# One word and the first rows ahead of the branch, and the MLP weights converted in pairs

## What is computed

```
h = RMSNorm(x);  [gB|gC|xA|xL|gL] = h @ w_in              # 1024 -> 5 x 512
outA = gB * conv3(gC * xA)                                # mixer A
outB = RG_LRU(conv4(xL) + b) * gelu(gL)                   # mixer B: h_t = a_t h_{t-1} + b_t
x = x + concat([outA, outB]) @ w_out
x = x + relu(RMSNorm(x) @ w_up)^2 @ w_down                # 4096 hidden columns
y = RMSNorm(x)
```

## Time and profile before

| | |
|---|---|
| median of 3 runs | 910.05 us (909.71 to 910.27) |
| the profiled execution | 909.05 us |
| its slowest core, 6 | span 907.5 us |
| even cores (0, 2, 4, 6) | 903.0 to 907.5 us |
| odd cores (1, 3, 5, 7) | 899.8 to 902.1 us |
| TensorE busy on core 6 | 839.3 us (92%) |
| VectorE, ScalarE, GpSimd | 425.2, 376.3, 184.9 us |
| queue of GpSimd's DMAs, share of 16 engines | 23.2% (33.30 MB) |
| queue of SyncE's DMAs | 42.4% (111.76 MB) |

### The profile page before, as it was taken

The page is one execution under the profiler, slowest core; times in us unless marked ns, Lnnn a source line. Parts: engine busy times, 40 slices in busy tenths (PEclk is TensorE's granted clock), DMA queues, the critical chain, the costliest instruction groups (busy, mean ns, idle before and its releaser), DMA issues.

```text
span 907.5 us, 15041 instructions; the slowest of 8 cores (899.8 to 907.5 us)
## 1 busy us (share of the span) xinstructions
PE 839.3 (92%) x4392; PEld 428.5 (47%) x4464; DVE 425.2 (47%) x722; ACT 376.3 (41%) x754; POOL 184.9 (20%) x307
## 2 busy tenths in 40 slices
PE   2679789699999999999999999999999899999995
PEld 2444345255564444444444444555445455446542
DVE  4698886663301210636665434575315477514112
ACT  4578738552331000554942134583205485205301
POOL 4132240234453000232100013120003212003200
PEclk9799889899999999999999999999999999999998
DMA  8999999999888534685553369565248852778751
GB/s 237 205 180 215 214 117 130 134 180 177 163 182 168 145 96 126 241 318 172 141 149 84 117 164 300 163 166 161 84 151 254 267 159 73 233 198 271 206 163 73
DMA packets 80441, 158.26 MB, mean 174 GB/s; under 512 B 9184, under 2 KB 9312, under 8 KB 80352
## 3 DMA queue, kind: packets, MB, share of 16 engines
q1 hardware_dynamic: 61632, 111.76, 42.4%
q0 software_dynamic: 15264, 33.30, 23.2%
q10 hardware_dynamic: 3456, 12.14, 4.1%
HBM read 165.75 MB, written 32.57 MB: 219 GB/s over the span
## 4 chain that ended last, share of the span: by engine, by line
PE 82%; DMA 8%; DVE 4%; issue 3%; ACT 2%; POOL 0%; POOLq 0%; DVEq 0%; ACTq 0%; SPq 0%
PE ps L1037 28%; PE ps L1087 27%; PE ps L780 12%; PE ps L989 7%; DMA sb_ring<-wscr 4%; PE ps L776 3%; DMA sb_uT<-wall 3%; PE ps L1079 2%; PE ps L697 1%; PE ps L1097 1%; DMA sb_xsl<-xp 1%; PE ps L855 1%; ACT sb_t_rig L532 1%; PE ps L1074 1%; DVE sb_t_xc L882 1%
## 5 line engine op out<-in xcount | busy, mean ns | idle before, releaser
L1037 PE MATMUL ps<-sb_hT,sb_ring 128*128 128x512 bf16 (+2 forms) x1050 | 194.3, 341 | 6.2 <-DVE sb_a_pb L535 4.3
L532 ACT ACTIVATE sb_junk<-sb_xsl 128x1024 bf16<-128x1024 f32 (+1 forms) x59 | 59.6, 1010 | 269.7 <-DVE sb_xsl L535 256.6
L535 POOL TENSOR_TENSOR sb_uT<-sb_rl 128x512 bf16<-128x512 bf16 (+1 forms) x80 | 83.0, 1038 | 418.4 <-ACT sb_stat L532 272.7
L532 ACT ACTIVATE sb_rl<-ps 128x512 bf16<-128x512 f32 (+2 forms) x192 | 98.1, 525 | 142.2 <-PE ps L1037 127.8
L1037 PEld LDWEIGHTS ps<-sb_hT,sb_ring 128*128 128x128 bf16 x1064 | 104.4, 99 | 91.3 <-issue 8.4
L535 DVE TENSOR_TENSOR sb_xsl<-ps,sb_xsl 128x512 f32<-128x512 f32 (+1 forms) x60 | 46.1, 794 | 200.7 <-PE ps L1087 139.9
L1087 PE MATMUL ps<-sb_ring,sb_uT 128*128 128x512 bf16 x576 | 138.5, 379 | 0.8
L1087 PE MATMUL ps<-sb_uS,sb_uT 128*128 128x512 bf16 x423 | 95.7, 379 | 0.5
L1037 PE MATMUL ps<-sb_hT,sb_uS 128*128 128x512 bf16 (+1 forms) x466 | 92.6, 354 | 0.3
L1087 PEld LDWEIGHTS ps<-sb_ring,sb_uT 128*128 128x128 bf16 x592 | 57.6, 98 | 67.8
L780 PE MATMUL ps<-sb_hT,sb_ring 128*128 128x512 bf16 (+1 forms) x369 | 81.8, 367 | 5.0 <-DMA sb_ring<-wscr 4.6
(11 more groups left out here) (100 smaller groups left out, 841.7 us busy)
## 6 DMA issues: line engine op xcount, KB each, us to landing
sb_ring<-wscr SPq DMA_DIRECT2D x240, 256.0 KB, 3.5
sb_uS<-wscr SPq DMA_DIRECT2D x160, 256.0 KB, 3.0
wscr<-wall POOLq DMA_DIRECT2D x64, 256.0 KB, 10.8
sb_xsl<-xp ACTq DMA_DIRECT2D x18, 512.0 KB, 8.7
yp<-sb_xsl POOLq DMA_DIRECT2D x13, 512.0 KB, 7.9
sb_uT<-wall POOLq DMA_DIRECT2D x16, 256.0 KB, 24.1
wscr<-sb_uT SPq DMA_DIRECT2D x16, 256.0 KB, 14.4
sb_wout<-wout POOLq DMA_DIRECT2D x4, 512.0 KB, 13.1
```

Of the source, the lines that this page charges most:

```text
L532: return OP("act", dur, lambda e: e.activation(out=out, in_=in_, func=func, **kw), rd_, wr_)
L535: return OP(eng, dur, lambda e: e.tensor_tensor(out=out, in0=in0, in1=in1, op=op), rd_, wr_)
L1037: return lambda slot: [lambda e, kc=kc: e.matmul(out=bank_ap(b, q.N), lhsT=slot[:, kc * 128:(kc + 1) * 128], rhs=h_ap(q, True, kc, 0, q.N) ...
```

## The change

1. **Ahead of the branch.** `W.lead` emits the first instruction of `g_par` (the load of `par`) and the first of the new `g_head` (1 MB of rows) before anything else. `cut` holds how many entries of each engine's program these are; `emit` puts them between the read of the word and the branch. On ScalarE these are two DMAs, on the other engines nothing.
2. **The first rows.** A new input `head` (128 x 6144) holds the first 3 MB of rows in the order in which they are used: on even cores the two blocks of S and the four of M0, on odd cores the 2 MB of L0 and the two blocks of S. It is loaded by four DMAs (1, 1, 0.5 and 0.5 MB) in place of six on even cores (2 of `xs`, 4 of `xp`), and of four on odd cores.
3. **Pairs.** The chunks of `w_up` and `w_down` lie in `wall2` as 32 pairs of 128 x 2048 with rows padded to 2064, and are converted to the scratch `wscr2` by one DMA each. Both chunks of a pair share one buffer in the planner. Ring loads still take one chunk, now as rows of 2 KB at a stride of 4 KB. The planner's size of such a transfer is 0.94 for a pair instead of 0.52 for a chunk. The chunks of `w_in` and `w_out` stay as they are.

```diff
         def f(e):
+            n = cut[name]
             r = e.alloc_register("side")
             e.reg_load(r, side[0:1, 0:1])
+            put(e, arms[0].prog[name][:n])
             with e.If_eq(r, 0):
-                put(e, name, arms[0])
+                put(e, arms[0].prog[name][n:])
...
+        for i in range(CH_UP + 1, NCHUNK, 2):
+            scr_b[i] = scr_b[i - 1]
...
+        def scr_ap(chunk):
+            p, h = divmod(chunk - CH_UP, 2)
+            return wscr[chunk] if chunk < CH_UP else wscr2[p, :, h * 1024:(h + 1) * 1024]
...
-                S.dma("sp", ap, wscr[chunk], [scr_b[chunk]], [buf], "ring")
+                S.dma("sp", ap, scr_ap(chunk), [scr_b[chunk]], [buf], "ring")
...
-                    yield DMA("pool", wscr[chunk], wall[chunk, :, 0:1024], [], [scr_b[chunk]], "cv", 0.52)
+                    p = (chunk - CH_UP) // 2
+                    yield DMA("pool", wscr2[p], wall2[p, :, 0:2048], [], [scr_b[chunk]], "cv", 0.94)
...
+        def g_head():
+            for k in range(6):
+                P_x.free.remove(k)
+            for k, n in ((0, 2), (2, 2), (4, 1), (5, 1)):
+                yield DMA("act", xsl[:, k * D:(k + n) * D], head[:, k * D:(k + n) * D], [], [xsl_b[k + i] for i in range(n)], "x", 0.52 * n)
...
-            for t in chain:
+            for t in chain[2:]:
...
-        W.spawn(g_conv(order), 500)
+        setup, conv, pars, rows = g_setup(), g_conv(order), g_par(), g_head()
+        for gen, n in ((pars, 1), (rows, 1)):
+            W.lead(gen, n)
+        cut = {e: len(S.prog[e]) for e in S.ENG}
```

More of the change, by code:

```diff
@@ L143, in check_no_deadlock, with emit, put @@
             raise RuntimeError("static deadlock: " + "; ".join(msg))
-def emit(nc, arms, side):
-    def put(e, name, S):
-        for waits, fns, inc in S.prog[name]:
+def emit(nc, arms, cut, side):
+    def put(e, part):
+        sem = arms[0].sem
+        for waits, fns, inc in part:
             for k, v in waits:
-                e.wait_ge(S.sem[k], v)
+                e.wait_ge(sem[k], v)
             ins = None
@@ L156, in put @@
             if inc is not None:
-                ins.then_inc(S.sem[inc[0]], inc[1])
+                ins.then_inc(sem[inc[0]], inc[1])
     def make(name):
         def f(e):
+            n = cut[name]
             r = e.alloc_register("side")
             e.reg_load(r, side[0:1, 0:1])
+            put(e, arms[0].prog[name][:n])
             with e.If_eq(r, 0):
-                put(e, name, arms[0])
+                put(e, arms[0].prog[name][n:])
             with e.Else():
-                put(e, name, arms[1])
+                put(e, arms[1].prog[name][n:])
         return f
@@ L355, in _emit, with lead @@
                 b.tw = land
+    def lead(self, gen, n):
+        s, val = Strand(gen, -99, 0), None
+        pace, self.PACE = self.PACE, {}
+        while n:
+            s.req, val = gen.send(val), None
+            if s.req[0] == "get":
+                val = s.req[1].take(s.req[2])
+            else:
+                self._emit(s, self._start(s.req))
+                n -= 1
+        self.PACE = pace
     def run(self):
@@ L381, in dout @@
         return nc.dram_tensor(name, list(shape), dt, kind="ExternalOutput").ap()
-    xp, xl, xs = din("xp", [NF, D]), din("xl", [128, 8 * NF]), din("xs", [256, D])
+    xp, xl, head = din("xp", [NF, D]), din("xl", [128, 8 * NF]), din("head", [128, 6 * D])
     side_d = din("side", [1, 1], mybir.dt.int32)
-    wall = din("wall", [NCHUNK, 128, WPAD])
+    wall = din("wall", [CH_UP, 128, WPAD])
+    wall2 = din("wall2", [(NCHUNK - CH_UP) // 2, 128, 2 * 1024 + 16])
     wout_d = din("wout", [128, 8 * 1024])
@@ L391, in build_program @@
     stp_d, sts_d = dout("stp", [128, 24]), dout("sts", [128, 96])
-    wscr = nc.dram_tensor("wscr", [NCHUNK, 128, 1024], BF16).ap()
+    wscr = nc.dram_tensor("wscr", [CH_UP, 128, 1024], BF16).ap()
+    wscr2 = nc.dram_tensor("wscr2", [(NCHUNK - CH_UP) // 2, 128, 2 * 1024], BF16).ap()
     es = ExitStack()
@@ L641, in arm @@
         Ms = tiles("M", xp, SECOND if second_half else FIRST, 20, 10, yp)
-        Ss = mk_tile("S", "S", xs, 0, 256, 4, 1.5, ys, 0)
+        Ss = mk_tile("S", "S", head, 0, 256, 4, 1.5, ys, 0)
         Ms[-1].last = True
@@ L645, in arm @@
         chain = Ls[0:1] + [Ss] + Ls[1:] + Ms
+        assert [t.J if not t.lean else 4 for t in chain[:2]] in ([4, 2], [2, 4])
         def xap(k):
@@ L650, in xap @@
             return xsl[:, k * D:(k + 1) * D]
+        def g_head():
[3 more added lines that the diff above has]
+                yield DMA("act", xsl[:, k * D:(k + n) * D], head[:, k * D:(k + n) * D], [], [xsl_b[k + i] for i in range(n)], "x", 0.52 * n)
+            if second_half:
+                Ls[0].xs, Ss.xs = {0: [0, 1], 1: [2, 3]}, {0: 4, 1: 5}
+            else:
+                Ss.xs, Ms[0].xs = {0: 0, 1: 1}, {0: 2, 1: 3, 2: 4, 3: 5}
+            for t in chain[:2]:
+                for _ in t.xs:
+                    W.mark("x" + t.name)
         def g_xloads():
-            for t in chain:
+            for t in chain[2:]:
                 for u in range(t.loads if t.lean else 0):
@@ L1165, in g_state @@
             out_events.append(S.last_dma)
-        order = [12, 13, 14, 15] + [16, 8, 4, 0, 17, 9, 5, 1, 18, 10, 6, 2, 19, 11, 7, 3] + list(range(CH_UP, NCHUNK))
-        W.spawn(g_setup(), -20)
-        W.spawn(g_conv(order), 500)
-        W.spawn(g_par(), -19)
-        W.spawn(g_xloads(), -10)
+        order = [12, 13, 14, 15] + [16, 8, 4, 0, 17, 9, 5, 1, 18, 10, 6, 2, 19, 11, 7, 3] + list(range(CH_UP, NCHUNK, 2))
+        setup, conv, pars, rows = g_setup(), g_conv(order), g_par(), g_head()
+        for gen, n in ((pars, 1), (rows, 1)):
+            W.lead(gen, n)
+        cut = {e: len(S.prog[e]) for e in S.ENG}
+        for gen, prio in ((setup, -20), (conv, 500), (pars, -19), (rows, -11), (g_xloads(), -10)):
+            W.spawn(gen, prio)
         W.spawn(g_norm1s(), -1)
@@ L1188, in arm @@
         S.check_no_deadlock()
-        return S, W
+        return S, W, cut
     with es:
         arms = [arm(False), arm(True)]
-        emit(nc, [a[0] for a in arms], side_d)
+        emit(nc, [a[0] for a in arms], arms[0][2], side_d)
+        assert arms[0][2] == arms[1][2]
     return nc, arms[0][1], arms[1][1]
@@ L1215 @@
     shared = {
-        "wall": f(np.pad(wall, ((0, 0), (0, 0), (0, WPAD - 1024)))), "wout": f(f(w_out[0]).reshape(8, 128, 1024).transpose(1, 0, 2).reshape(128, 8192)),
+        "wall": f(np.pad(wall[:CH_UP], ((0, 0), (0, 0), (0, WPAD - 1024)))),
+        "wall2": f(np.pad(wall[CH_UP:].reshape(-1, 2, 128, 1024).transpose(0, 2, 1, 3).reshape(-1, 128, 2048), ((0, 0), (0, 0), (0, 16)))),
+        "wout": f(f(w_out[0]).reshape(8, 128, 1024).transpose(1, 0, 2).reshape(128, 8192)),
         "wbd": f(wbd.reshape(8, 128, 128).transpose(1, 0, 2).reshape(128, 1024)), "gf": f(norm_f_g),
@@ L1219 @@
     sca, slc, slh = f(state_conv_a[0]), f(state_lru_conv[0]), f(state_lru_h[0])
+    tall = lambda a: a.reshape(-1, 128, D).transpose(1, 0, 2).reshape(128, -1)
     in_maps = []
@@ L1225 @@
         rows[:len(mine)] = mine
+        wide = f(np.concatenate([x_prompt[s, a:a + n].reshape(n, 8, 128).transpose(2, 1, 0).reshape(128, 8 * n)
+                                 for a, n in zip(np.cumsum((0,) + SKIP), SKIP)], axis=1))
+        few = tall(x_sample[4 * c:4 * c + 4].reshape(256, D))
         st = np.concatenate([sca[4 * c:4 * c + 4].reshape(8, 512), slc[4 * c:4 * c + 4].reshape(12, 512), slh[4 * c:4 * c + 4]], axis=0)
@@ L1230 @@
             "xp": rows,
-            "xl": f(np.concatenate([x_prompt[s, a:a + n].reshape(n, 8, 128).transpose(2, 1, 0).reshape(128, 8 * n)
-                                    for a, n in zip(np.cumsum((0,) + SKIP), SKIP)], axis=1)),
-            "xs": f(x_sample[4 * c:4 * c + 4].reshape(256, D)),
+            "xl": wide,
+            "head": f(np.concatenate([wide[:, :4096], few] if hf else [few, tall(rows[:512])], axis=1)),
             "side": np.full((1, 1), hf, np.int32),
```

## The result

The changed kernel takes 938.81 us against 909.95: a ratio of 1.0315 with a 95% interval of 1.0296 to 1.0334. The forecast was 906.8 us with a range up to 915, so it failed in sign and in size. One of the four executions of the changed kernel took 1019.28 us, with half of the cores at a lower granted clock (0.85 to 0.88); such executions stand in no comparison here, and the other three took 937.5 to 939.9 us.

A forecast was written before the change was run, and what follows sets the result against it. The even arm was taken to bound the kernel, with conversions on its path from 124 to 180 us. 909.05 - 0.3 (start) - 3.0 (pairs) = 905.75, plus 1.0 for the median: 906.8 us; range 899.5 to 915, the forecast's own 904 to 908.2.

The forecast's parts named there:

- What bounds the kernel: Whole kernel: even cores end last (core 6 at 907.5 us); conversions from 124 to 180 us cost them 7.1 us.
- The planner now orders everything anew; plus or minus 2 us: Pairs, whole program: the planner's new order was worth plus or minus 2 us that no row can price.
- Waits and queues, cost 0: Pairs, SyncE's and GpSimd's queues: first chunk late by 2.2 to 2.8 us, hidden by the planner's 20 us; cost 0.
- What a pair costs: Conversions to DRAM: a paired chunk takes 2.0 us of the 16 engines against 2.22, 10% less.
- The 3.0 us: Even cores' ring stall, 124 to 180 us: pairs shrink it by 3.0 us, between 0.9 and 6.6.
- rival 2: Whole kernel: no difference, a pair costs twice a chunk and start gains vanish; 909.0 to 910.5 us, chance 0.21.
- Rival 1: Ring loads, 130 to 176 us: longer turns land one 7 us later; 913.8 us, within slower's chance of 0.25.
- The signs that I named for the profile after: Profile after: ring loads at 124 to 160 us landing in 9 to 12 us support the forecast, 16 to 20 rival 1.
- The part ahead of the branch: Start: odd cores' rows 4 us sooner (1.5 to 7), off the path, 0 us of the metric; even cores 0.1 us.
- the 1.2 us: Even cores' start: fewer row DMAs free ScalarE 1.2 us sooner, mostly lost waiting for weights; 0.3 us taken.
- all rows must land before the late chunk anyway: Even cores' start: why 8 KB row packets beside 4 KB conversions could lose at most 0.5 us.
- slower: Whole kernel: 912 to 915 us, by rival 1 or an order that falls badly; chance 0.25.

## Why the prediction was wrong

**What bounds the kernel: right, and short by a stage.** The even arm sets the time, and the transfers around conversions are its weak place; both held. But I took the stretch from 124 to 180 us for the one place where conversions sit on the path, since there TensorE already waited. The new wait arose at 105 us, where before there was none: its first link is the write-back of `w_in` chunks at 76 us, a step that I did not price at all.

**"The planner now orders everything anew; plus or minus 2 us": the step that failed.** This was the term that decided. `PACE` counts transfers, and a transfer had become two chunks: that stands in the code and asks for no chip. The planner let 18 chunks stand where 13 stood. By the run with 19 single chunks there such an amount costs 1.4%, 13 us, where I allowed 2. The word "everything" was wrong as well: pairs alone leave the even cores' other engines in their order, but for 3 places of ScalarE's, and the loss is all there.

**"Waits and queues, cost 0": wrong for the same reason.** I argued that the planner leaves 20 us between the landing of a conversion and its use. It does, but the loads that came late were not of converted up chunks; they were of written-back `w_in` chunks, which share SyncE's queue. Its model gives a load fixed weights for the queues that are busy beside it, whatever their rows, and has no turns by the row. What was queued behind the write-back is what I had named (all later ring loads and TensorE behind them), in the wrong place and at 0.

**What a pair costs: no saving.** I took 10% less per chunk, from single stretches of 3 us. Over 30 us (90 to 120) on the four even cores a conversion took 131 to 133 us of engine time per MB in the changed kernel and 124 to 126 with short rows in the same order; 127 to 129 and 122 to 127 in the two runs with pairs at the order of before; 125 to 129 with six more single chunks, 117 to 125 before. So the long row costs some 2 to 7% more, not less. My 136 for single chunks came from one core and 3 us, where cores 0 and 2 showed 122 and 120. The 3.0 us had no source, and rival 2's statement, a pair costs twice a chunk, was the nearest.

**Rival 1: right mechanism, wrong size and place.** It gave 913.8 for long turns. The long row at the order of before measures 1.0056, 5 us (3.7 were given). Ring loads from 124 to 160 us land there in 14.3 to 15.5 us after 12.5 to 12.7, where the rival had 19.7. The packets show the turns: 285 to 285, 1467 to 1465, 1564 to 1563. I had left open whether turns go by row or transfer; they go by row. The Trainium skill's sentence in "DMA: Bandwidth & Descriptors", Queues, rings and completion order, that an engine goes round its queues held here. Its figure of a whole packet of 9 to 17 descriptors before a change did not show: with 256 rows against 128 in a transfer the packets in the trace still stood one to one, where turns by the transfer would have given two to one.

**What is left open.** At the order of before, the long row measures 0.56% and the larger amount 1.40%; the pairs alone, with both, 3.01%, so 1% more than the sum. In these three runs the even cores' other engines keep one order (3 places of ScalarE's apart), so a new order is not the reason. The row's length explains little of it: it costs 0.5% with few chunks ahead (1.0056 against 1.0003) and 0.8% with many (1.0315 against 1.0237). What remains is the grouping when much is ahead: a pair can be read only as a whole. Short-row pairs with 18 chunks at 92 us and 22 at 109 cost 2.37%, single chunks with 19 and 22 cost 1.40%, which fits, though the order and the start differ there too. That the grouping does it was argued and not tried alone.

**The signs that I named for the profile after.** Ring loads from 124 to 160 us land in 10.5 to 11.9 us on the even cores of the changed kernel, with 2107 to 2676 packets on q1 where 765 to 940 were. I had given such a landing as support for the forecast. It says nothing of what came before it: on core 2 no pair is issued between 109 and 146 us, so the backlog runs out in that stretch. The sign that came true is the last one, another wait on the even arm.

**The start.** The part ahead of the branch did on the odd cores what I said: VectorE starts on the rows at 17.25 us instead of 20.38, inside 13 to 19, and the last 1 MB of the second L tile's rows is issued at 25.1 us in place of 33.5. On core 7, after:

```profile
2.54 0.38 ACTq L112 DMA_DIRECT2D sb_par<-par  x1
2.95 9.22 ACTq L112 DMA_DIRECT2D sb_xsl<-head  x4
...
17.25 4.65 DVE L563 TENSOR_SCALAR sb_hT<-sb_xsl,sb_par 128x512 bf16<-128x512 f32 x8
```

The odd cores end at 892 to 901 us in the start alone, 1 to 9 us sooner, and it is off the path as said. In the changed kernel they give it all back.
On the even cores, after (core 6):

```profile
2.93 2.61 ACTq L112 DMA_DIRECT2D sb_xsl<-head  x4
5.58 2.30 ACTq L112 DMA_DIRECT2D sb_xsl<-xp  x2
7.96 1.28 ACT L556 ACT_TABLE_LOAD   x1 [7.96 <-issue]
```

Two DMAs fewer do not free ScalarE sooner: the four from `head` take 0.65 us each and not the 0.56 that I took, the last two 1.15 in place of 0.66, and the table load stands at 7.96 as before. So the 1.2 us were not hidden, they did not exist. And the wait of tile S for `w_in` grew from 7.3 us to 12.7 in the start alone, 5 us where I bounded the loss at 0.5; yet core 6 ends at 906.6 us there after 907.5, so it is won back, and where was not traced. Core 6 in the start alone:

```profile
36.16 1.87 PE L809 MATMUL ps<-sb_hT,sb_uT 128*128 128x256 bf16 x8 [12.68 <-DMA sb_uT<-wall]
```

From 5 to 25 us the row queue has 61.8% of the engines there after 50.3% before, the conversions 34.7% after 46.0%. My argument that all rows must land before the late chunk anyway was wrong as arithmetic, or the engines lost time; the row length of the M0 loads is not the reason, by the run that halves them (11.7 us). This stays open.

**The forecast's chance.** A quarter stood on slower, in a case that ended at 915. The range was too narrow because it priced one mechanism at one place and gave the changed order on GpSimd's queue 2 us.

## What to carry to other kernels

When transfers are merged, look for every count that is kept in transfers: a limit of six under way lets twice the bytes stand ahead. Price a bulk queue by what the latency-bound queue gets beside it, and do so at each stage where that queue has work, not only where a wait already shows. The amount ahead is worth trying as a number of its own, and with the order of the other engines held: six more chunks cost 1.4% here, three fewer gave 0.6% with the new start and nothing in the order that came with the shorter row loads. Where the planner also moved the other engines, the run could not say.

## What the runs showed of the hardware

- With both queues filled, the 16 DMA engines took one row from each by turns, for rows of 1024 against 1024 elements as for 2048 against 1024, whatever the size of the transfer (285 to 285, 1467 to 1465, 1564 to 1563 packets; in the starts of 2545 packets one queue was never more than 6 ahead). SyncE's queue moved 0.52 MB in 10 us beside rows of 4 KB.
- A ring load of 256 KB landed in 2.7 us where GpSimd's queue was all but empty (core 6 before, 300 to 340 us, 15 loads), in 12.6 us beside some conversions, in 31.9 us beside a steady backlog of rows of 1024, and in 37.4 us in the changed kernel, beside rows of 2048.
- A conversion from DRAM to DRAM cost, from 90 to 120 us, 117 to 129 us of engine time per MB written with rows of 1024 elements and 127 to 133 with rows of 2048. From 124 to 160 us rows of 512 cost 179 us per MB on core 0 and 182 on core 6 (77.2% for 2.48 MB, 76.8% for 2.43), where rows of 1024 cost 159 and 170.
- Merging row loads into DMAs of 1 MB did not save issue time at the queue's end: the DMAs issued behind them took 1.15 us each in place of 0.66.
